# Stick-breaking attention: the causal mask copied into the score banks by ScalarE

## The reference

```
z = einsum("bhtd,bhsd->bhts", qb, kb) * scale          # scores
mask = s_idx < t_idx                                   # key strictly before query
log_keep = where(mask, log_sigmoid(-z), 0.0)
tail = cumsum(log_keep, axis=3, reverse=True)
between = concatenate([tail[..., 1:], zeros], axis=-1)
a = where(mask, exp(log_sigmoid(z) + between), 0.0)
out = einsum("bhts,bhsd->bhtd", a, v)
```

## Time and profile before

| | us |
|---|---|
| median of 3 runs | 1509.68 (1508.86 to 1509.8) |
| the profiled execution | 1509.62 |
| span of its trace | 1507.7 |
| TensorE busy | 1491.2 (99%) |
| ScalarE busy | 676.0 (45%) |
| VectorE busy | 849.4 (56%) |
| GpSimd busy | 806.4 (53%) |

### The profile page before, as it was taken

How to read it: one execution, slowest core, us unless ns; L and a number is a source line. 1 busy time by engine, 2 the same in 40 slices (tenths; PEclk the granted TensorE clock), 3 DMA queues, 4 the chain that set the end, 5 groups by cost and what they waited for, 6 DMA issues and landing times.

```text
span 1507.7 us, 19993 instructions
## 1 busy us (share of the span) xinstructions
PE 1491.2 (99%) x6808; PEld 1235.1 (82%) x6808; DVE 849.4 (56%) x1292; ACT 676.0 (45%) x1019; POOL 806.4 (53%) x988
## 2 busy tenths in 40 slices
PE   9999999999999999999999999999999999999997
PEld 6888888888888888888788888888788888888886
DVE  7998996555555511169874655646745555511145
ACT  6787786433333322247463543635633333322243
POOL 5343335666666655467365253551566666655452
PEclk9999999999999999999999999999999999999999
DMA  4121112322222422243133322321232222332221
GB/s 178 57 70 56 42 56 69 101 98 95 97 97 97 142 97 96 70 168 98 56 141 99 106 89 91 133 98 30 96 103 92 97 97 97 119 111 97 92 84 56
DMA packets 42806, 142.14 MB, mean 94 GB/s; under 512 B 4224, under 2 KB 10496, under 8 KB 42752
## 3 DMA queue, kind: packets, MB, share of 16 engines
q1 hardware_dynamic: 41104, 138.69, 27.2%
q10 hardware_dynamic: 1648, 2.74, 0.5%
HBM read 139.32 MB, written 2.10 MB: 94 GB/s over the span
## 4 chain that ended last, share of the span: by engine, by line
PE 92%; DVE 3%; POOL 2%; ACT 1%; DMA 1%; issue 0%; SPq 0%; POOLq 0%; DVEq 0%; ACTq 0%
PE bank L595 26%; PE bank L599 26%; PE bank L598 26%; PE bank L873 3%; PE bank L877 3%; PE bank L878 3%; PE bank L673 2%; POOL wl L557 2%; PE bank L653 1%; DVE xl L1118 1%; PE bank L654 1%; PE bank L684 1%; PE bank L683 1%; DMA raw<-in_w 1%; DVE sumsq L1112 0%
## 5 line engine op out<-in xcount | busy, mean ns | idle before, releaser
L541 POOL TENSOR_TENSOR wl<-raw,wh 128x256 fp32r<-128x256 f32 x752 | 616.6, 852 | 474.7 <-ACT wh L1695 474.7
L595 PE MATMUL bank<-xh,wh 128*128 128x512 f32 (+1 forms) x1160 | 451.6, 389 | 1.7 <-POOL wl L541 0.7
L599 PE MATMUL bank<-xh,wl 128*128 128x512 f32 (+1 forms) x1160 | 450.3, 388 | 0.0
L598 PE MATMUL bank<-xl,wh 128*128 128x512 f32 (+1 forms) x1160 | 450.2, 388 | 0.0
L1695 ACT ACTIVATE wh<-raw 128x1024 fp32r<-128x1024 f32 (+1 forms) x212 | 235.0, 1108 | 479.2 <-PE bank L595 388.8
L595 PEld LDWEIGHTS bank<-xh,wh 128*128 128x128 f32 x1160 | 218.0, 188 | 47.8 <-POOL wl L541 1.6
L599 PEld LDWEIGHTS bank<-xh,wl 128*128 128x128 f32 x1160 | 217.9, 188 | 45.0
L598 PEld LDWEIGHTS bank<-xl,wh 128*128 128x128 f32 x1160 | 217.9, 188 | 43.7
L557 POOL TENSOR_TENSOR wl<-raw,wh 128x256 fp32r<-128x256 f32 x160 | 128.4, 834 | 186.1 <-ACT wh L1695 186.1
L1138 DVE TENSOR_TENSOR x<-x,bank 128x512 f32<-128x512 f32 x56 | 38.5, 688 | 253.2 <-PE bank L599 253.2
L598 PE MATMUL bank<-yl,wh 128*128 128x512 f32 x352 | 137.0, 389 | 0.0
(11 more groups left out here) (224 smaller groups left out, 2342.6 us busy)
## 6 DMA issues: line engine op xcount, KB each, us to landing
raw<-in_w SPq DMA_DIRECT2D x180, 512.0 KB, 3.2
raw<-in_w SPq DMA_DIRECT2D x32, 704.0 KB, 4.0
rc<-in_w SPq DMA_DIRECT2D x16, 512.0 KB, 3.8
w_end<-in_w SPq DMA_DIRECT2D x8, 512.0 KB, 4.0
rb<-in_w SPq DMA_DIRECT2D x8, 512.0 KB, 6.2
x<-in_xT SPq DMA_DIRECT2D x4, 512.0 KB, 6.7
pin<-in_pT ACTq DMA_DIRECT2D x2, 512.0 KB, 3.3
outT<-x ACTq DMA_DIRECT2D x2, 384.0 KB, 3.9
```

The lines of the kernel that those rows point to most:

```text
L541: last = nc.gpsimd.tensor_tensor(wl[:, slot, cols], part[:, cols], wh[:, slot, cols].bitcast(F32), ALU.subtract)
L595: first = mm(out, ah_, bh_, start=start, stop=False, skip_group_check=True)
L598: mm(out, ah_, bl_, start=False, stop=False, skip_group_check=True)
L599: return mm(out, al_, bh_, start=False, stop=stop, skip_group_check=True)
```

## The change

For every head but the first the mask matmul is gone. In its place stands a new ScalarE copy, `mask_scores(j)`: after ScalarE has read bank `Z[j]` for the weights of head s, it writes `masked` (an SBUF tile of 512 columns, -1e30 at the masked places of the first 128 columns, zero in the rest) over it, 128, 256, 384 or 512 columns wide. TensorE's product for head s + 1 then adds to what stands there (`start=False`), and waits for `z_masked` of the block rather than for `a_full`. The first head keeps the mask matmul. Head 15 has no head after it, so 15 times 4 copies are added, and 60 matmuls of 128 columns removed. `masked` is filled once: GpSimd clears columns 128 to 511, ScalarE copies the first 128 from the constants. The diff:

```diff
+            masked = sb("masked", [T], F32, ph)
...
+            nc.gpsimd.memset(masked[:, P:T], 0.0).then_inc(mask_zeros, 1)
+            pool.wait_ge(mask_zeros, 1)
             with pool.Fori(0, PAIRS) as i:
...
                 for jj, j in enumerate(reversed(range(TB))):
-                    if not isinstance(s, int) or s >= 1:
-                        pe.wait_ge(a_full, 4 * s - 4 + jj + 1)
+                    opening = isinstance(s, int) and s == 0
+                    if not opening:
+                        pe.wait_ge(z_masked, 4 * s - 4 + jj + 1)
                     keys = slice(j * P, (j + 1) * P)
                     z = Z[j][:, 0:T - j * P]
                     k_ = k_pack[half]
-                    mm(z, k_[:, par_, keys], qh[half][:, par_, j * P:T], start=True, stop=False, skip_group_check=True)
-                    mm(z, k_[:, par_, keys], q_pack[half][:, par_, j * P:T], start=False, stop=False,
-                       skip_group_check=True)
-                    mm(z[:, 0:P], ident_r[:], maskneg[:], start=False, stop=True,
-                       skip_group_check=True).then_inc(z_done, 1)
+                    mm(z, k_[:, par_, keys], qh[half][:, par_, j * P:T], start=opening, stop=False, skip_group_check=True)
+                    last = mm(z, k_[:, par_, keys], q_pack[half][:, par_, j * P:T], start=False, stop=not opening,
+                              skip_group_check=True)
+                    if opening:
+                        last = mm(z[:, 0:P], ident_r[:], maskneg[:], start=False, stop=True, skip_group_check=True)
+                    last.then_inc(z_done, 1)
...
+                def mask_scores(j):
+                    if more or half == 0:
+                        copy(Z[j][:, 0:T - j * P], masked[:, 0:T - j * P], z_masked)
+
...
                 act.wait_ge(both_full, s + 1)
+                if first:
+                    act.wait_ge(mask_ready, 1)
                 for jj in range(TB + 1):
...
                     if jj:
                         act.wait_ge(a_full, 4 * s + jj)
                         copy(ah[j + 1][:], sp[j + 1][:], a_high)
+                    if jj > 1:
+                        mask_scores(j + 2)
+                mask_scores(0)
                 if more and half == 0:
                     split_qk(p + 1, 0, 1 - par_)
...
             opening_high(0)
+            act.wait_ge(cst_loaded, 16)
+            act.wait_ge(mask_zeros, 1)
+            copy(masked[:, 0:P], cst[:, C_MASK - C_TRI:C_MASK - C_TRI + P], mask_ready)
             tile_high(ATT_RING + 1)
```

More of the change, by code:

```diff
@@ L252, in program @@
         q_zeros = sem("q_zeros")
+        mask_zeros, mask_ready, z_masked = sem("mask_zeros"), sem("mask_ready"), sem("z_masked")
         z_done, z_exp, z_ln = sem("z_done"), sem("z_exp"), sem("z_ln")
```

## The result

| | before | after |
|---|---|---|
| median, us | 1509.70 (1508.86 to 1509.80, 4 runs) | 1520.59 (1519.96 to 1520.74, 4 runs) |
| span of the trace, us | 1507.7 | 1518.6 |
| pair of the loop, us (mean of six) | 27.52 | 28.95 |

The account below looks back on a forecast made before the run. In the loop only TensorE's work set the time before the change. Delays of 1.04 (first pair), 9.06 (six transitions) and 1.21 (last pair), together 11.3 us, on 1509.62 gave 1520.9 us; own range 1515 to 1526, wider range 1512 to 1527.

Parts of the forecast that it names:

- 1: Half 0, ScalarE: three copies of 1.25 us don't fit idle time, moving `qh`, `oh` and half 1's softplus phase; no TensorE stall.
- 2: VectorE's softplus of half 1, running without a pause to `att_tmp`: all of it moves by 1.25 us.
- 3: ScalarE before `k_pack` in half 1: it waits for `att_tmp`, so `k_pack` moves by the full 1.25 us.
- 4: ScalarE's weights phase of half 1: last Exp moves from 108.57 to 110.03, last mask copy ends at 112.78.
- 5: TensorE, block 0 of the next pair's half 0 scores: values start at 113.39 instead of 111.88, 1.51 us later each pair.
- The price of a copy: ScalarE copies into banks: 0.21, 0.31, 0.43 and 0.51 us by width, 1.46 us for each head.
- what the removal saves: TensorE's scores: 0.10 us for each mask matmul, 0.40 for each head, 6.0 in all were TensorE still the bound everywhere.
- rival A: Block 0 of half 0's scores: the chain has room, all 6.0 us are gained, 1503.6 us; chance 0.07.
- Rival B: ScalarE and VectorE catch up half 0's 1.25 us before half 1; 3.4 us lost, 1513.0 us; chance 0.12.
- Rival C: Delay also reaches `cumulate` of half 0: another 1.25 us for each of 7 pairs, 1529.7 us; chance 0.05.
- Rival D: TensorE's clock in the loop drops because of new gaps; one pair at the lower level adds 27.5 us, above 1540; chance 0.03.
- sign on `cumulate`: Half 1, before line 680: perhaps some tenths of a us of TensorE idle time, released by VectorE's late last `spl`.

Follow-up runs that it names:

- the run with block 3 alone: Against the kernel before, only the 128-column block j = 3 is seeded by ScalarE, in every head but the first; other blocks keep the mask matmul: 1508.28 us.
- the run above: Kernel before with the 60 ScalarE copies added at the changed kernel's places, into an SBUF tile nobody reads; all mask matmuls kept: 1517.12 us, ratio 1.0049.
- the run for half 0 only: Changed kernel with only half 0's scores seeded, copies in half 1's weights phase; half 1's scores keep the mask matmul: 1511.55 us, ratio 1.0013 to before.
- the run for half 1 only: Changed kernel with only half 1's scores seeded, copies in half 0's weights phase; half 0's scores keep the mask matmul: 1514.69 us, ratio 1.0033 to before.
- blocks 3 and 2: Against the kernel before, blocks j = 3 and j = 2 seeded by ScalarE in every head but the first; others keep the mask matmul: 1509.64 us, ratio 1.0000.
- the last two runs: Against before: ScalarE seeds block 3, VectorE blocks 2 and 1 of half 1 heads, 1509.10 us; the same without VectorE's copies in the first pair, 1506.99 us.

## Why the prediction was right

The forecast was 1520.9; the measured median is 1520.59. Its steps, with the times of the changed trace put on the scale of before (scores of half 1 start at 99.02 there and at 96.65 before, so 2.37 is taken off):

| step | forecast | measured |
|---|---|---|
| 1: `qh` of half 0 | 96.76 | 99.12 - 2.37 = 96.75 |
| 1: softplus phase of half 1 | 98.58 | 100.94 - 2.37 = 98.57 |
| 2: `att_tmp` | 105.08 + 1.25 = 106.33 | 108.70 - 2.37 = 106.33 |
| 3: `k_pack` | 105.79 + 1.25 = 107.04 | 109.41 - 2.37 = 107.04 |
| 4: last Exp of half 1 | 110.03 | 112.39 - 2.37 = 110.02 |
| 4: last mask copy ends | 112.78 | 115.12 - 2.37 = 112.75 |
| 5: values | 113.39 | 115.73 - 2.37 = 113.36 |

The rows are of the changed kernel, on ScalarE and VectorE:

```profile
99.12 1.28 ACT L1702 ACTIVATE qh<-att_tmp 64x512 fp32r<-64x512 f32 x2
100.30 0.61 ACT L1702 ACTIVATE oh<-of 64x512 f32 x1
100.94 0.56 ACT L1797 ACTIVATE sp<-bank 128x128 f32<-128x128 f32 x2
...
108.70 0.68 DVE L1211 SCALAR_TENSOR_TENSOR att_tmp<-bank,rstd 128x512 f32<-128x512 f32 x1
```

The terms of the sum are read from where TensorE stands at the end of the first pair, of the loop, and of the last scores:

```profile
57.82 0.39 PE L690 MATMUL bank<-ah,v_pack 128*128 128x512 f32 x1
...
231.50 0.39 PE L690 MATMUL bank<-ah,v_pack 128*128 128x512 f32 x1
...
243.48 0.40 PE L600 MATMUL bank<-oh,wh 128*128 128x512 f32 x1
```

Before, these stood at 56.84, 221.96 and 232.58 (the trace of before, and the earlier trace rows). So the first pair loses 0.98 (forecast 1.04), the six pairs of the loop 8.56 (forecast 9.06), which is 1.43 each against 1.51, and the last 1.36 (forecast 1.21): 10.9 together, where the forecast had 11.3. In the pair followed (1.45), block 0 starts 0.08 earlier than forecast (0.03 because the copies end earlier, 0.05 in the hand-over, which takes 0.05 and not 0.10), but its two matmuls take 0.56 and not 0.51; another 0.03 is gained from the values to the scores of half 1 (86.76 to 99.02 is 12.26 us, 84.36 to 96.65 before is 12.29). These terms partly cancel, so that the sum comes within 0.4 us of the measured loss is in part luck; that the path and its copies are right is not. One sum of the prediction is wrong: the chances that it leaves outside 1512 to 1527 add up to 0.21, not 0.18. The price of a copy was right: start to start 0.20, 0.31, and 0.93 for two, against 0.21, 0.31 and 0.94. So was what the removal saves where TensorE doesn't wait: scores of half 1 take 1.27 us (99.02 to 100.29), as the values did, and in the run with block 3 alone each matmul removed is worth 0.11 us. The 56 ns that the Trainium skill gives for back-to-back matmuls of 128 columns ("TensorE: Matmul & The Clock Gate", section "Wait — 56ns, not 53.3ns?") is half of that.

What the prediction missed is a second wait. It said in its first paragraph that TensorE "only needs the Exp of 108.57 there", and gave it 2.15 us of room. That holds for the scores; the values right behind them need `al`, with 0.88 us. It did not change the forecast, since the path through the mask copies ends 0.6 us later in each pair; that the missed path happened to be the shorter one is luck. But it made the argument against rival A too weak, and it broke the two expectations that rested on the same omission, by 7 and by 4 us. Even with copies that nobody waits for the kernel loses 7.5 us (the run above, which keeps the mask matmuls): two thirds of the loss are due to what the copies push back, and only the last third to the waits for the copies themselves.

Rival A (room in the chain): refuted by both paths. Rival B (the delay of half 0 is caught up): refuted, `att_tmp` and `k_pack` moved by the full 1.25; removing half 0's copies (the run for half 0 only) gave back 9 of the 10.9 us. ScalarE alone does catch up: its `q_pack`, before and after,

```profile
103.92 1.29 ACT L1695 ACTIVATE q_pack<-qh 64x512 fp32r<-64x512 f32 x2
...
106.48 1.29 ACT L1702 ACTIVATE q_pack<-qh 64x512 fp32r<-64x512 f32 x2
```

moves by 0.19 only (106.48 - 2.37 = 104.11), since a wait of 0.94 us before the last `wh` is gone. It is VectorE that has no pause and carries the whole delay on, and ScalarE then waits for it. Rival C (the other half too): TensorE has no idle time before line 680 in half 0, and ScalarE still waits for it there, 2.77 us (3.60 before). Rival D: the granted clock of the run is 0.998 in both kernels; the gaps, up to 0.7 us, did not lower it. The forecast's sign on `cumulate` was right too: an idle time of 0.37 us in half 1, where the last `spl` comes late,

```profile
108.83 0.49 PE L680 MATMUL bank<-sph,negtri 128*128 128x512 f32 x1 [0.37 <-DVE spl L1105]
```

which costs nothing by itself, since the mask copies come later still. Not tried was the same set of copies at other places in ScalarE's queue, for instance behind `qh` and `oh` in half 0; it would test the part that the order plays directly.

## What to carry to other kernels

Work taken off the engine that sets the time is worth something only if the work that replaces it comes early enough; follow the receiving engine's queue through a whole cycle of the loop, instruction by instruction, and list for every instruction of the bound engine the slack of everything it waits for, the ones behind the edited place too. A pause of an engine is usable only where it stands, however little the engine is busy on average (ScalarE 78% here, VectorE 92%): 0.24 us on ScalarE took one 128-column copy and 0.83 us on VectorE two more, and this part of the change pays 2.7 us, while all of it costs 10.9. Where two halves of an edit share the same slack, their costs don't add: 1.9 and 5.0 alone, 10.9 together.

## What the runs showed of the hardware

A ScalarE copy of the float32 tile `masked` into a bank took 0.27, 0.38, 0.49 and 0.59 us for 128, 256, 384 and 512 columns (means of 15 rows each, changed kernel); the same copy into the SBUF tile `spare` took 0.30, 0.41, 0.52 and 0.62 (means of 15, the run with copies that nobody waits for). That is what these runs show of the rule of the Trainium skill that ScalarE is faster towards PSUM ("ScalarE: Activation LUTs", section "Step-by-step: what each stage is for"): 0.03 us in length, and nothing from start to start (into banks 0.20 for 128 columns, 0.31 for 256 and 0.93 for the last two together; into `spare` 0.20, 0.30 and 0.93), which is what a full queue pays. A mask matmul of 128 columns, 0.06 us from its start to the next one's, is worth 0.11 us when it is removed between larger ones (two fewer in each pair shorten it from 27.52 to 27.30 us, 84.17 to 111.47 in the run with block 3 alone). TensorE started a matmul 0.05 to 0.06 us after the end of the ScalarE copy that it waited for, and 0.12 to 0.14 us after the end of VectorE's last `al` (113.83 to 113.97; 113.05 to 113.17 in the run for half 1 only; 111.60 to 111.73 with blocks 3 and 2). Matmuls with `start=False` added to the -1e30 and zeros that ScalarE, and VectorE in the last two runs, had written into the banks, and the attention stayed the reference's; the first head's matmuls had written every one of these columns before.
